# Recurrent gates of a two-layer streaming encoder: one 64-row product per head on two row groups, and a later slot for the attention values

## The reference

```
u  = causal_conv(xa);  ub = u in 16 heads of 64 channels
r  = sigmoid(einsum('bshi,hij->bshj', ub, w_r) + b_r)
i  = sigmoid(einsum('bshi,hij->bshj', ub, w_i) + b_i)
log_a = -8 * r * softplus(-lambda);  a = exp(log_a)
h  = scan(a, sqrt(1 - exp(2 log_a)) * i * u);  y = h * silu(ga)
```

## Time and profile before

| | us |
|---|---|
| median of 3 runs | 1915.05 (1914.8 to 1917.05) |
| the profiled execution, its own time | 1916.71 |
| its span, first to last instruction | 1914.8 |
| TensorE busy | 1890.6 (99%) |
| VectorE, ScalarE, GpSimd busy | 1172.4 (61%), 992.4 (52%), 393.5 (21%) |
| mean granted TensorE clock | 0.999 |

### The profile page before, as it was taken

The page is one execution under the profiler, slowest core; times in us unless marked ns, Lnnn a source line. Parts: engine busy times, 40 slices in busy tenths (PEclk is TensorE's granted clock), DMA queues, the critical chain, the costliest instruction groups (busy, mean ns, idle before and its releaser), DMA issues.

```text
span 1914.8 us, 27900 instructions
## 1 busy us (share of the span) xinstructions
PE 1890.6 (99%) x11048; PEld 1020.4 (53%) x11048; DVE 1172.4 (61%) x1555; ACT 992.4 (52%) x1912; POOL 393.5 (21%) x266
## 2 busy tenths in 40 slices
PE   7999999999999999999999999999999999999998
PEld 4446765455455664544454477554554555655443
DVE  6677556587436777654367765655873468776432
ACT  5674454465334666543356645544662356765421
POOL 0212021142222332111001130112332222321110
PEclk9999999999999999999999999999999999999999
DMA  6224334443334655434222252354333344554421
GB/s 191 88 88 150 104 106 138 121 122 90 109 105 131 155 128 165 112 132 146 59 67 88 72 166 89 106 150 120 110 105 110 113 137 126 148 138 116 165 84 44
DMA packets 264747, 224.68 MB, mean 117 GB/s; under 512 B 88400, under 2 KB 253226, under 8 KB 264618
## 3 DMA queue, kind: packets, MB, share of 16 engines
q1 hardware_dynamic: 264618, 222.90, 39.3%
HBM read 182.96 MB, written 2.16 MB: 97 GB/s over the span
## 4 chain that ended last, share of the span: by engine, by line
PE 87%; DVE 4%; ACT 3%; issue 2%; POOL 2%; DMA 1%; SPq 1%; DVEq 0%; ACTq 0%; POOLq 0%
PE PS L591 85%; POOL X L1694 1%; DVE Y L1338 1%; DMA X<-X 1%; PE PS L695 1%; DVE X L1338 1%; ACT Y L1077 1%; DVE wsp L1335 1%; SPq L512 1%; DMA stage<-w_in 1%; ACT Y L1078 0%; SPq L564 0%; POOL Y L1694 0%; PE PS L819 0%; ACT wsp L1000 0%
## 5 line engine op out<-in xcount | busy, mean ns | idle before, releaser
L591 PE MATMUL PS<-hT,wsp 128*128 128x512 f16 (+2 forms) x4968 | 1083.2, 377 | 1.0 <-ACT hT L981 1.0
L591 PEld LDWEIGHTS PS<-hT,wsp 128*128 128x128 f16 x4968 | 479.5, 98 | 562.8 <-issue 13.6
L1335 DVE SCALAR_TENSOR_TENSOR wsp<-stage,wsp 128x2048 f16<-128x2048 f32 x148 | 352.9, 2384 | 164.8 <-ACT wsp L1000 162.6
L591 PE MATMUL PS<-ys,wsp 128*128 128x512 f16 x1536 | 339.4, 379 | 0.0
L1000 ACT ACTIVATE wsp<-stage 128x2048 f16<-128x2048 f32 x148 | 281.3, 1901 | 46.6 <-PE PS L591 44.7
L591 PEld LDWEIGHTS PS<-ys,wsp 128*128 128x128 f16 x1536 | 149.4, 98 | 178.4 <-issue 4.1
L591 PE MATMUL PS<-wsp,hT 128*128 128x256 f16 x1728 | 193.2, 273 | 0.0
L591 PEld LDWEIGHTS PS<-wsp,hT 128*128 128x128 f16 x1728 | 168.6, 98 | 22.7 <-issue 2.3
L1003 ACT ACTIVATE X<-PS 128x512 f32<-128x512 f32 (+1 forms) x120 | 68.4, 593 | 140.5 <-PE PS L591 108.2
L1694 POOL TENSOR_TENSOR X<-X,K 128x1024 f32<-128x1024 f32 x26 | 62.7, 2412 | 351.3 <-DMA X<-X 351.3
L1694 POOL TENSOR_TENSOR M<-M,T 128x512 f32<-128x512 f32 x48 | 67.4, 1407 | 292.1 <-DVE T L1335 292.1
(11 more groups left out here) (195 smaller groups left out, 1974.4 us busy)
## 6 DMA issues: line engine op xcount, KB each, us to landing
stage<-w_in SPq DMA_DIRECT2D x120, 1024.0 KB, 5.0
stage<-w_branch SPq DMA_DIRECT2D x32, 1024.0 KB, 5.3
X<-X SPq DMA_DIRECT2D x120, 128.0 KB, 2.4
stage<-w_out SPq DMA_DIRECT2D x8, 1024.0 KB, 5.4
Y<-sums SPq DMA_DIRECT2D x8, 512.0 KB, 6.3
M<-sums SPq DMA_DIRECT2D x8, 512.0 KB, 5.9
Y<-Y SPq DMA_DIRECT2D x24, 128.0 KB, 3.2
xres<-x SPq DMA_DIRECT2D x4, 512.0 KB, 6.7
```

Of the source, the lines that this page charges most:

```text
L591: return pe.matmul(o, a, b, start=start, stop=stop, skip_group_check=True)
L1335: return dve.scalar_tensor_tensor(out=o, in0=a, scalar=c, in1=b, op0=op0, op1=op1)
```

## The change

Each head gets one product for both of its gates: its stationary operand has the head's 64 rows and 128 columns, 64 for one gate and 64 for the other. The two heads of a tile lie on partitions 0 to 63 and 64 to 127, so their products use two row groups and two banks. For head 0 the columns are r, i and for head 1 they are i, r, so r comes out on its own partitions for both, and i on the other half. ScalarE reads i from the other half of the bank, with the bias of the other half (the host swaps the halves of `lru_b_i`). Each tanh becomes two of 64 partitions. The clearing by GpSimd goes. `dt_taken` is given by VectorE's first read of bank 4, and TensorE waits for that instead of `dta_ready`. SyncE waits for `out_sq` itself in layer 1. `VALUES_AT` goes from 8 to 10.

```diff
-VALUES_AT = 8
+VALUES_AT = 10
...
-        wbd = Y[:, 3072:5120].rearrange("p (t r n) -> p t r n", t=8, r=2)
+        wgate = Y[:, 3072:4096].rearrange("p (t r n) -> p t r n", t=8, r=2)
...
-                sp.wait_ge(s["wbd_zero"], at("wbd_zero", 1, layer))
+                if layer > 0:
+                    sp.wait_ge(s["out_sq"], at("out_sq", 4, layer - 1))
                 for r, w in enumerate((w_r, w_i)):
                     for o in range(2):
-                        sp.dma_start(wbd[HD * o:HD * o + HD, :, r, HD * o:HD * o + HD],
+                        sp.dma_start(wgate[HD * o:HD * o + HD, :, (r + o) % 2, :],
...
                             if t == 0:
-                                pe.wait_ge(s["wbd_in"], at("wbd_in", 64, layer))
-                                pe.wait_ge(s["dt_raw"], at("dt_raw", 1, layer))
-                                pe.wait_ge(s["dta_ready"], at("dta_ready", 1, layer))
+                                pe.wait_ge(s["wgate_in"], at("wgate_in", 64, layer))
+                                pe.wait_ge(s["dt_taken"], at("dt_taken", 1, layer))
...
-                            mm(PS[:, 4 + 2 * u, :], wbd[:, t, 0, :], cbuf[:, u, :], True, True)
-                            mm(PS[:, 5 + 2 * u, :], wbd[:, t, 1, :], cbuf[:, u, :], True, True).then_inc(s["lru_gates"], 1)
+                            for o in range(2):
+                                rows_of = slice(HD * o, HD * o + HD)
+                                last = mm(PS[:, 4 + 2 * u + o, :], wgate[rows_of, t].rearrange("p r n -> p (r n)"), cbuf[rows_of, u, :], True, True)
+                            last.then_inc(s["lru_gates"], 1)
...
-                            link(act.activation(rbuf[:, u, :], PS[:, 4 + 2 * u], ACT.Tanh, scale=0.5, bias=halfA[:, A_BR + t:A_BR + t + 1]))
+                            head0, head1 = slice(0, HD), slice(HD, P)
+                            act.activation(rbuf[head0, u, :], PS[head0, 4 + 2 * u], ACT.Tanh, scale=0.5, bias=halfA[head0, A_BR + t:A_BR + t + 1])
+                            link(act.activation(rbuf[head1, u, :], PS[head1, 5 + 2 * u], ACT.Tanh, scale=0.5, bias=halfA[head1, A_BR + t:A_BR + t + 1]))
...
-                            act.activation(wbuf[:, u, :], PS[:, 5 + 2 * u], ACT.Tanh, scale=0.5, bias=halfA[:, A_BI + t:A_BI + t + 1])\
+                            act.activation(wbuf[head0, u, :], PS[head1, 4 + 2 * u], ACT.Tanh, scale=0.5, bias=halfA[head1, A_BI + t:A_BI + t + 1])
+                            act.activation(wbuf[head1, u, :], PS[head0, 5 + 2 * u], ACT.Tanh, scale=0.5, bias=halfA[head0, A_BI + t:A_BI + t + 1])\
                                 .then_inc(s["lru_w"], 1)
...
-                        link(stt(spw[:, 0, 0:64].rearrange("p (c j) -> p c j", c=ST), PS[:, 4, 0:64].rearrange("p (c j) -> p c j", c=ST),
-                                 IWS, bias, ALU.mult, ALU.add))
+                        stt(spw[:, 0, 0:64].rearrange("p (c j) -> p c j", c=ST), PS[:, 4, 0:64].rearrange("p (c j) -> p c j", c=ST),
+                            IWS, bias, ALU.mult, ALU.add).then_inc(s["dt_taken"], 1)
+                        dve.wait_ge(s["dt_taken"], at("dt_taken", 1, layer))
...
-                if layer > 0:
-                    pool.wait_ge(s["out_sq"], at("out_sq", 4, layer - 1))
-                pool.memset(wbd.rearrange("p t r n -> p (t r n)"), 0.0).then_inc(s["wbd_zero"], 1)
```

More of the change, by code:

```diff
@@ L120 @@
     "dec_ready": 1, "df_lo": 32, "vd_hi": 8, "df_hi": 32, "df_turned0": 256, "df_turned1": 256, "df_a": 32, "df_e": 32, "df_m": 32, "df_n": 4, "df_nT": 8, "df_o": 32,
-    "df_or": 32, "df_s": 32, "df_sq": 4, "df_y": 8, "dt_raw": 1, "cs_rows": 1, "rows_out": 16, "seg_in0": 64, "seg_in1": 64, "dta_ready": 1, "dve_free": 100,
+    "df_or": 32, "df_s": 32, "df_sq": 4, "df_y": 8, "dt_raw": 1, "dt_taken": 1, "cs_rows": 1, "rows_out": 16, "seg_in0": 64, "seg_in1": 64, "dta_ready": 1, "dve_free": 100,
     "fin_ss": 4, "fin_sum": 4, "first_cols": 2, "first_hi": 2, "first_in": 16, "first_lo": 2, "first_par": 3,
@@ L129 @@
     "ssd_y": 8, "step_in": 16, "sw_T": 16, "sw_Ta": 16, "sw_e": 16, "sw_m": 16, "sw_n": 16, "sw_o": 16, "sw_s": 16,
-    "sw_vE": 3, "sw_y": 16, "tile_done": 160, "wbd_in": 64, "wbd_zero": 1, "x_new": 4, "xn_T": 16, "xn_ready": 4,
+    "sw_vE": 3, "sw_y": 16, "tile_done": 160, "wgate_in": 64, "x_new": 4, "xn_T": 16, "xn_ready": 4,
     "xt_done": 10, "xt_read": 10, "y_hi": 32, "y_lo": 32, "yb_hi": 2, "yb_lo": 2,
@@ L335, in program @@
         names = ["cols_in", "first_in", "step_in", "second_in", "rows_in", "first_turned", "first_cols", "first_hi",
-                 "first_lo", "first_par", "xn_ready", "stored", "wbd_zero", "wbd_in", "post_in", "load0", "load1",
+                 "first_lo", "first_par", "xn_ready", "stored", "wgate_in", "post_in", "load0", "load1",
                  "hi_done", "lo_done", "tile_done", "act_free", "dve_free", "gate_ready", "act_chain", "dve_chain",
-                 "pool_chain", "xn_T", "h_hi", "h_lo", "dt_raw", "sp_in", "sp_exp", "dta_ready", "cs_done",
+                 "pool_chain", "xn_T", "h_hi", "h_lo", "dt_raw", "dt_taken", "sp_in", "sp_exp", "dta_ready", "cs_done",
                  "cs_ready", "dec_ready", "lru_par", "conv_first", "lru_gates", "lru_a", "lru_v", "lru_w", "lru_a2",
@@ L1835 @@
     tiles = lambda v: v.reshape(L, -1, P)
+    heads_swapped = lambda v: np.roll(tiles(v), HD, axis=2)
     li = np.array([[0.8 - 0.6 * math.exp(-0.3 * l)] for l in range(L)])
@@ L1839 @@
         "w_r": a["lru_w_r"], "w_i": a["lru_w_i"],
-        "cols_a": np.concatenate([tiles(a[n]) for n in ("pre_norm_g", "b_merge", "lru_conv_w", "lru_conv_b", "lru_b_r",
-                                                         "lru_b_i", "lru_lambda")], axis=1),
+        "cols_a": np.concatenate([tiles(a[n]) for n in ("pre_norm_g", "b_merge", "lru_conv_w", "lru_conv_b", "lru_b_r")]
+                                 + [heads_swapped(a["lru_b_i"]), tiles(a["lru_lambda"])], axis=1),
         "cols_b": np.concatenate([tiles(a[n]) for n in ("ssd_conv_w", "ssd_conv_b", "ssd_norm_g", "diff_norm_g")], axis=1),
```

2 lines of the change are left out of this document (1 added, 1 removed).

## The result

The changed kernel takes 1932.81 us (median of 4 runs, 1930.47 to 1933.77), the kernel before beside it 1914.92 (4 runs): a ratio of 1.0086, 95% interval 1.0074 to 1.0098, some 16.5 us slower by the ratio (the two medians lie 17.9 apart). The forecast was 1916.2 with a range up to 1922. It was wrong.

The account below looks back on a forecast made before the run. A ScalarE-VectorE ring was taken as already slower than 99% busy TensorE in the gates' slots, living on a lead. Gates +9.0 and values' move −7.9 gave +1.1 us on the median 1915.05: 1916.2 us, range 1907 to 1922.

Parts of the forecast that it names:

- The price of an added activation: ScalarE's gates: four more activations per block at 0.57 us each, 2.28 per block, 9.12 for a layer's four blocks.
- 9.0: Gates' part in us: slot 10 starts 5.0 later in layer 0 and 4.0 later in layer 1.
- The ring, its lead and its idles: ScalarE and VectorE, 24.60 us per two slots against TensorE's 24.1; lead 2.63 at slot 10; idles 0.68, 0.77 used up.
- layer 1's earlier start: ScalarE starts layer 1's gates at 990.55 instead of 992.30, −1.75 us, once the parameters are ready.
- TensorE's 1.4 us per block: Gate block of paired 64-row products takes 2.02 us instead of 3.44; 5.6 us per layer, worth nothing while the ring is behind.
- `dta_ready`: TensorE's wait for it in layer 1 goes, giving 2.5 us that only lengthen the wait at slot 10.
- The values' move: Attention: values two steps later remove TensorE's waits on line 1080, but for one, and a clock fall: 7.9 us gained.
- the values' step gives nothing: Rival: the exponentials slip with the values, so 1924.1 us; little or no gain from the step had chance 0.14.
- 1.7 us for the clock: Layer 1 behind slot 50: 3.4 us at 1.2 GHz taken as gone, 1.7 us of the values' gain.
- the clock falls at the new waits: Rival: covered at slot 8, but behind slot 10 a fall costs 1.7 us per layer, 1919.5; chance 0.18.
- activations hide: Rival, ring of slots 2 to 10: added activations cost nothing or the ring yields; 17.1 us gained, 1898; chance 0.15.
- row groups don't overlap: Rival: a gate block takes 3.7 us, but slot 10 still waits, same time; chance 0.45 together with the forecast.

Follow-up runs that it names:

- run 3: Kernel before, products untouched, with each tanh of the gates made in two halves on its own partitions: 1934.06 us, ratio 1.0091.
- run 5: Kernel before with both gates' tanh split into halves, ordered so that equal halves stand side by side: 1931.22 us, ratio 1.0083.
- run 6: Kernel before with only the input gate's tanh split into two of 64 partitions: 1922.56 us, ratio 1.0033.
- run 7: Changed kernel with products also cut into 64 columns (four quarters) and one whole tanh for the recurrence gate: 1919.24 us, ratio 1.0018 to the kernel before.
- run 4: Kernel before, with the gates' first product waiting for `dt_taken` instead of `dta_ready`: 1912.93 us, ratio 0.9986.
- run 1: Kernel before with only `VALUES_AT` moved from 8 to 10: 1915.97 us, ratio 0.9994.
- run 2: Changed kernel with `VALUES_AT` back at 8, the gates' part alone: 1932.93 us, ratio 1.0084 to the kernel before.
- run 11: Kernel before with `dt_taken`, swapping copies ahead of the second block's transposes, and the values' product at step 9: 1910.59 us, ratio 0.9972.

## Why the prediction was wrong

**The price of an added activation: the step that failed.** "I take 0.57 each, 2.28 per block (bounds: 0, if the halves were free, and 4 × 0.67 = 2.7)." It is 3.31 per block, above the upper bound, because neighbours suffer too. Per tile: a second half adds a distance of 0.70 for each gate, the first tanh of the next tile follows 0.14 later (0.71 for 0.57), and the first half behind a whole activation 0.12 later. With 3.31 the prediction's own sum gives 13.24 in place of 9.12, and 9.0 becomes 9.0 + 2 × 4.12 = 17.2 us for the gates; the run of that part alone lost 16 us. The bound was wrong in form: a duration bounds a distance only if nothing else keeps two instructions apart. The copies of the earlier trace rows, from which I had that partitions don't count, could have shown the distance. They alternate between the two halves of the partitions; a pair of them in order of time, kernel before:

```profile
632.55 2.13 ACT L1003 ACTIVATE X<-X 64x1024 f16<-64x1024 f32 x2 [1.47 <-DVE X L1338]
```

Two of 1.055 us in 2.13: no overlap between two halves, while whole tanh overlap by 0.10. The Trainium skill (ScalarE: Activation LUTs, What ACT_TABLE_LOAD costs) says that activations back to back overlap by about 93 ns; the whole ones agree, and for neighbours on different halves the runs show 0.01 or none (0.67 to 0.71 apart, 0.68 long).

**The ring, its lead and its idles: right.** Both idles used, the lead of 2.63, layer 1's earlier start and the rigidity hold to a few tenths in layer 0 of all five kernels. That a layer loses four times what a block gains, less a fixed room, is shown by runs 3, 5, 6 and 7 and by the changed kernel. For layer 1 the sum is right to 0.2 us in the changed kernel and up to 1.5 too low in others, by what is added between the two rings. TensorE's 1.4 us per block was right (1.5 measured) and worth nothing, as said; the 0.05 us in it for a first weight load came from no row, and nothing here shows it. `dta_ready`: 2.5 us for TensorE, shown by run 4, and covered in the changed kernel but for ScalarE's earlier start.

**The values' move: the second step that failed.** −7.9 us forecast, −1.1 measured with an interval that holds 0. The waits were priced as if TensorE paced these slots; the waits' sum was the same afterwards. I had looked at ScalarE's read of the values alone, not at what hangs on it. With 13.24 for 9.12 in both layers and −1.1 for −7.9 the forecast's sum gives +16.1 us, against 16.5 measured. The rival "the values' step gives nothing", with 0.14, was what happened; that the later start of the products lengthens the second ring is argued from run 1's rows, and that the ring exists is shown by them.

**1.7 us for the clock** should not have been a term of the sum. The stretch at 0.50 behind slot 50 is absent in run 4's profile, which has the wait of 1.04 us in front of that slot's second block, TensorE in order of time:

```profile
1561.09 0.51 PE L591 MATMUL PS<-X,Y 128*128 128x128 f16 x6 [1.04 <-ACT small L1079]
```

and its stretch (columns as above):

```profile
1561.00:1567.00 6.00, 5.91 (x37) 3.08 (x38) 4.93 (x7) 4.29 (x12) 0.00 (x0) 1.00 0.35 111
```

But run 4 has only this wait, where the kernel before had 0.83 us in front of the first block too; no other profile here has both. So whether the fall hung on the pair of waits or came by chance is not shown. The 21 timed executions of the kernel before that runs 1 to 4 are compared with differ among themselves: six have a mean clock of 0.998 and take 1918.0 us on average, the other fifteen 0.999 or 1.000 and 1915.5. A median already holds what is usual of such falls. The profiled execution was 1.7 us above it, and this stretch was a likely part of that.

The rival "the clock falls at the new waits" was right about the fall. In the changed kernel's profile it costs nothing, since all four stretches are covered; but behind slot 10, where the rival put its 1.7 us, run 2's profile has exactly this loss, in one layer of two. The rivals "activations hide" and "row groups don't overlap" fall.

What stays open: which of the second ring's pieces, VectorE or ScalarE, would have to be shortened for the head's end; why run 11's waits fell and its time didn't; when the clock falls; the 0.7 to 1.5 us between the two layers' rings that the sum misses in three kernels; and why the half behind a whole activation came 0.12 late in five kernels but not when only the input gate was split (0.71 there).

## What to carry to other kernels

Cost an instruction that is added to a busy in-order engine by the distance between starts beside the neighbours it will have, not by its duration; two halves of the partitions are two whole instructions and a little more. When TensorE is 99% busy, saving its time can be worth nothing for a long stretch of the schedule (slots 2 to 10 here, some 100 us): find the chain of the other engines and its lead over TensorE first. And before counting a wait as a gain, follow the chain through the wait's own end: if it has no piece of the waiting engine, the wait may come back somewhere else, here in the same sum. An effect of the clock seen in one execution is not a term of a sum on the median, until other executions show it.

## What the runs showed of the hardware

- Activations on 64 partitions take as long as on 128 (0.68 us for 512 elements), and two neighbours overlap by some 0.1 us only on the same half: starts 0.57 to 0.59 apart, against 0.67 to 0.71 where the half changes.
- Two row groups of 64 rows in fp32 run beside each other, and so do four quarters of 64 by 64: 8 or 16 products in 1.9 us, where 8 of 128 rows take 3.44.
- Reading PSUM on partitions 64 to 127 and writing SBUF on 0 to 63 in one activation costs nothing beside the same read in place: 0.68 us both, and the same distances.
- The clock does not follow from one wait: in one execution (run 2) it fell behind 2.07 us of idle at slot 10 of layer 0, where 36 matmuls then took 9.63 us, and not behind 2.08 us at the same place of layer 1, where they took 7.94. At the waits of 3.6 to 5.0 us in the changed kernel it was at 1.2 GHz in all four cases, in stretches of 3.4 to 6.8 us.
